# Gated attention in a two-model block: decays computed a head ahead, the gate's Silu behind the turned keys, state products first, level products mixed with eight blocks

## The reference, cut to what matters

```python
def gla_mixer(h, w_in, w_gate, b_gate, g_out, w_out):
    ...
    q, k, v, r, glr = jnp.split(proj, ...)
    log_a = jax.nn.log_sigmoid((glr @ w_gate + b_gate)) / GLA_TAU      # GLA_TAU = 16
    o = gla_chunked(q, k, v, log_a.reshape(B, S, H, DK))
    o = rmsnorm(o, g_out) * jax.nn.silu(r)
    return o.reshape(B, S, H * DV) @ w_out

def step(state, inp):                    # one chunk of gla_chunked
    qi, ki, vi, gi = inp
    b = jnp.cumsum(gi, axis=-2)
    o_inter = einsum(qi * exp(b), state)
    attn = einsum('bhik,bhjk,bhijk->bhij', qi, ki, exp(b_i - b_j, causal))
    o_intra = attn @ vi
    b_last = b[:, :, -1:, :]
    new_state = state * exp(b_last) + einsum(ki * exp(b_last - b), vi)
    return new_state, o_inter + o_intra
```

## Time and profile before

| | us |
|---|---|
| runs | 1488.01, 1482.47, 1490.82; median 1488.01 |
| profiled execution | 1484.64 |
| its span | 1482.9 |
| TensorE busy | 1389.9 (94%) |
| VectorE busy | 863.8 (58%) |
| ScalarE busy | 643.4 (43%) |
| TensorE's mean granted clock | 0.967 of full |

### The profile page before, as it was taken

How to read it: one execution, slowest core, us unless ns; L and a number is a source line. 1 busy time by engine, 2 the same in 40 slices (tenths; PEclk the granted TensorE clock), 3 DMA queues, 4 the chain that set the end, 5 groups by cost and what they waited for, 6 DMA issues and landing times.

```text
span 1482.9 us, 26632 instructions
## 1 busy us (share of the span) xinstructions
PE 1389.9 (94%) x9993; PEld 1267.9 (86%) x9993; DVE 863.8 (58%) x1635; ACT 643.4 (43%) x1171; POOL 14.9 (1%) x81
## 2 busy tenths in 40 slices
PE   5999999999999899999799987999999999899997
PEld 2988889888888799999677776999997778899996
DVE  0576667666533377777555544777775432775553
ACT  3455545455322255444554422545532332545542
POOL 4000000000000000000000000000000000000000
PEclk9899999999999999999999999899999999899998
DMA  8655446454491178879676822688797264476562
GB/s 303 187 154 159 131 125 185 143 156 144 126 304 53 42 216 261 265 218 296 180 225 201 250 63 65 183 262 271 226 281 264 91 166 121 133 224 182 155 185 86
DMA packets 400019, 270.00 MB, mean 182 GB/s; under 512 B 9914, under 2 KB 357424, under 8 KB 399936
## 3 DMA queue, kind: packets, MB, share of 16 engines
q1 hardware_dynamic: 399936, 268.83, 61.1%
HBM read 267.75 MB, written 1.05 MB: 181 GB/s over the span
## 4 chain that ended last, share of the span: by engine, by line
PE 84%; DVE 8%; ACT 4%; issue 2%; DMA 2%; SPq 1%; DVEq 0%; ACTq 0%
PE bank L738 18%; PE bank L739 18%; PE bank L740 17%; PE bank L724 6%; PE bank L792 4%; PE bank L695 2%; PE bank L1117 1%; DMA big<-in_w_ada 1%; PE bank L710 1%; PE bank L917 1%; PE bank L918 1%; PE bank L910 1%; PE bank L689 1%; DVE w_low L1789 1%; DVE h_parts L1805 1%
## 5 line engine op out<-in xcount | busy, mean ns | idle before, releaser
L738 PE MATMUL bank<-h_parts,w_high 128*128 128x256 f32 x1824 | 552.3, 303 | 17.1 <-DVE h_parts L1805 15.2
L739 PE MATMUL bank<-h_parts,w_high 128*128 128x256 f32 x1824 | 525.0, 288 | 0.0
L740 PE MATMUL bank<-h_parts,w_low 128*128 128x256 f32 x1824 | 524.4, 287 | 0.0
L1789 DVE TENSOR_TENSOR w_low<-w_raw,w_high 128x1024 fp32r<-128x1024 f32 (+2 forms) x324 | 362.0, 1124 | 108.6 <-ACT w_high L1310 96.9
L738 PEld LDWEIGHTS bank<-h_parts,w_high 128*128 128x128 f32 x1824 | 358.0, 196 | 35.3 <-issue 25.2
L739 PEld LDWEIGHTS bank<-h_parts,w_high 128*128 128x128 f32 x1824 | 359.6, 197 | 3.8 <-issue 3.5
L740 PEld LDWEIGHTS bank<-h_parts,w_low 128*128 128x128 f32 x1824 | 358.7, 197 | 0.0
L1310 ACT ACTIVATE w_high<-w_raw 128x1024 fp32r<-128x1024 f32 (+2 forms) x324 | 312.9, 973 | 63.4 <-PE bank L740 18.0
L738 PE MATMUL bank<-act_parts,w_high 128*128 128x256 f32 x528 | 150.1, 284 | 0.0
L1302 ACT ACTIVATE evac<-bank 128x256 f32<-128x256 f32 x140 | 53.9, 385 | 219.9 <-PE bank L740 195.9
L740 PE MATMUL bank<-act_parts,w_low 128*128 128x256 f32 x528 | 148.6, 281 | 0.0
(11 more groups left out here) (345 smaller groups left out, 1577.8 us busy)
## 6 DMA issues: line engine op xcount, KB each, us to landing
ada_w<-in_ada_w SPq DMA_DIRECT2D x48, 1024.0 KB, 6.2
w_raw<-in_ffn_w_in SPq DMA_DIRECT2D x88, 512.0 KB, 3.9
w_raw<-in_w_in SPq DMA_DIRECT2D x72, 512.0 KB, 3.9
w_raw<-in_w_ffn_in SPq DMA_DIRECT2D x44, 512.0 KB, 4.0
ada_w<-in_w_ada SPq DMA_DIRECT2D x16, 1024.0 KB, 7.1
w_raw<-in_gla_w_in SPq DMA_DIRECT2D x24, 512.0 KB, 6.4
w_raw<-in_ffn_w_out SPq DMA_DIRECT2D x32, 384.0 KB, 4.1
w_raw<-in_ffn_w_out SPq DMA_DIRECT2D x32, 320.0 KB, 3.6
```

Of the source, the lines that this page charges most:

```text
L738: pe.matmul(acc[:, 0:T], hi[:, n, :], x_parts[:, k, 0, :], start=k == 0, stop=False)
L739: pe.matmul(acc[:, 0:T], hi[:, n, :], x_parts[:, k, 1, :], start=False, stop=False)
L740: mm = pe.matmul(acc[:, 0:T], lo[:, n, :], x_parts[:, k, 0, :], start=False, stop=k == kb - 1)
L1789: dve.tensor_tensor(w_low[:, s, 0:m], w_raw[:, s, 0:m], w_high[:, s, 0:m].bitcast(F32), ALU.subtract)\
```

## The change

- VectorE's copy and subtractions become `decays(n)`. It is called once before the first head, and for head n + 1 in head n, behind the second state update (with a wait for it) and the low parts, before the wait for the norm. ScalarE's Exp becomes `decays(n)` too, called before the first head and then between the copy of block 5 and the Ln.
- VectorE computes `kd` before `qk2`.
- ScalarE's Silu and the two table loads move behind the copy of the turned keys.
- On TensorE the two state products (L1068) come before the level products. Block 3, eight k-steps, no longer follows them: one k-step is issued behind each of eight of the first eleven level products. `att_done` is signalled behind all of them.

```diff
                 products(G2)
                 rows2(1)
-                pe.wait_ge(S("scaled2"), 15 * (n - 1) + 2)
+                pe.wait_ge(S("scaled2"), 15 * (n - 1) + 1)
 ...
                 mm.then_inc(S("kd_turned"), 1)
                 products(G2)
                 rows2(2)
 
-                pe.wait_ge(S("scaled2"), 15 * n)
                 pe.wait_ge(S("tok2"), 2 * n)
-                for t in range(NT):
-                    for l in range(LEVELS):
-                        pe.matmul(bank[3 + t][:, l * CHUNK:(l + 1) * CHUNK], kt[:, l, tok[t]], qt[:, l, t, :], start=True, stop=True)
-                    mm = pe.matmul(bank[3 + t][:, 2 * T - 1:2 * T], qk2[:, tok[t]], ones[:, 0:1], start=True, stop=True)
-                mm.then_inc(S("att_done"), 1)
-
                 for c in range(2):
                     r = slice(c * CHUNK, (c + 1) * CHUNK)
                     if c == 1:
                         pe.wait_ge(S("kv_done"), 3 * (n - 1) + 1)
                     pe.matmul(bank[6][:, c * T:(c + 1) * T], kd_tok[r, 0, :], v_tok[r, 0, :], start=True, stop=True).then_inc(S("kv_done"), 1)
-                products(G2)
+                pe.wait_ge(S("scaled2"), 15 * n)
+                for t in range(NT):
+                    for l in range(LEVELS):
+                        pe.matmul(bank[3 + t][:, l * CHUNK:(l + 1) * CHUNK], kt[:, l, tok[t]], qt[:, l, t, :], start=True, stop=True)
+                        if t * LEVELS + l < NT * LEVELS - 1:
+                            products(1 if (t * LEVELS + l) % 3 < 2 else 0)
+                    mm = pe.matmul(bank[3 + t][:, 2 * T - 1:2 * T], qk2[:, tok[t]], ones[:, 0:1], start=True, stop=True)
+                mm.then_inc(S("att_done"), 1)
                 rows2(3)
 ...
@@ ScalarE
+            def decays(n):
+
+                act.wait_ge(S("expo"), 14 * n)
+                act.activation(expo, expo, ACT.Exp, scale=1.0 / TAU).then_inc(S("expo_done"), 1)
 ...
-                r = big[:, bass.ds(2 * i - 2, 2), :] if not isinstance(i, int) else big[:, 2 * i - 2:2 * i, :]
-                act.wait_ge(S("evacuated"), st_h2.done(i - 1, 1) + 3)
-                act.activation(r, r, ACT.Silu).then_inc(S("expo_done"), 1)
-                act.preload_act_table_set(LOG_EXP)
-                act.wait_ge(S("expo"), 14 * n)
-                act.activation(expo, expo, ACT.Exp, scale=1.0 / TAU).then_inc(S("expo_done"), 1)
 ...
                 act.activation(kd_tok.rearrange("p t d -> p (t d)"), bank[4][:, 0:NT * P], ACT.Copy).then_inc(S("tok2"), 1)
+                r = big[:, bass.ds(2 * i - 2, 2), :] if not isinstance(i, int) else big[:, 2 * i - 2:2 * i, :]
+                act.wait_ge(S("evacuated"), st_h2.done(i - 1, 1) + 3)
+                act.activation(r, r, ACT.Silu).then_inc(S("expo_done"), 1)
+                act.preload_act_table_set(LOG_EXP)
                 copies(5)
 ...
                 copies(6)
+                if gemm:
+                    decays(n + 1)
                 act.wait_ge(S("o2_sum"), n)
 ...
@@ VectorE
-                dve.tensor_tensor(qk2, q, k, ALU.mult).then_inc(S("scaled2"), 1)
-                dve.wait_ge(S("expo_done"), 2 * n)
+                dve.wait_ge(S("expo_done"), 2 * n - 1)
                 dve.tensor_tensor(kd, k, expo[:, 6 * T:7 * T], ALU.mult).then_inc(S("scaled2"), 1)
+                dve.tensor_tensor(qk2, q, k, ALU.mult).then_inc(S("scaled2"), 1)
 ...
                 if gemm and not last:
                     low(st_h2, i + 1, 0, IN_PARTS)
                     low(st_h2, i + 1, 1, IN_PARTS)
+                if gemm:
+                    dve.wait_ge(S("state2"), 3 * n)
+                    decays(i + 1)
                 dve.wait_ge(S("o2_rn"), 2 * n)
```

More of the change, by code:

```diff
@@ L1629, in _ @@
             head2(0, True, False)
+            decays(1)
             with act.Fori(1, H2 - 1) as i:
@@ L2190, in _, with decays @@
                 low(st_h2, 1, j, IN_PARTS)
-            def head2(i, gemm=True, last=False):
-                n, c = i, i - 1
-                cum = expo[:, 7 * T:8 * T]
+            cum = expo[:, 7 * T:8 * T]
+            def decays(n):
+                c = n - 1
                 dve.tensor_copy(cum, part(gb, c)).then_inc(S("expo"), 1)
@@ L2208, in head2 @@
                                   ALU.subtract).then_inc(S("expo"), 1)
+            def head2(i, gemm=True, last=False):
+                n, c = i, i - 1
                 dve.wait_ge(S("evacuated"), st_h2.done(c, 5) + 3)
                 q, k = qkv2[:, 0, :], qkv2[:, 1, :]
+                dve.wait_ge(S("expo_done"), 2 * n - 1)
+                dve.tensor_tensor(kd, k, expo[:, 6 * T:7 * T], ALU.mult).then_inc(S("scaled2"), 1)
                 dve.tensor_tensor(qk2, q, k, ALU.mult).then_inc(S("scaled2"), 1)
-                dve.wait_ge(S("expo_done"), 2 * n)
-                dve.tensor_tensor(kd, k, expo[:, 6 * T:7 * T], ALU.mult).then_inc(S("scaled2"), 1)
                 for l in range(LEVELS):
```

## The result

The changed kernel took 1500.76 us in the median of 4 runs (1499.91 to 1502.1), the kernel before 1485.45 us (1482.47 to 1490.82, 4 runs). The ratio is 1.0105 with a 95% interval of 1.0083 to 1.0127: slower by 15.6 us by the ratio, 15.3 between the medians. The forecast was 1500.7 us, +12.7, in a range of 1491 to 1507. One of the ten executions of `decays_ahead_only` further down (1494.86 us, at a mean granted clock of 0.915) fell into a slower state of the chip, and its ratio leaves it out. The profiled execution took 1502.1 us with a span of 1500.4, against 1484.64 and 1482.9.

A forecast was written before the change was run, and what follows sets the result against it. TensorE, on 84% of the chain that ended last, was taken to bound the kernel. Terms -6.5 -3.0 -2.9 +16.2 +4.8 +2.1 +1.45 +0.5 gave +12.7 us on 1488.0: 1500.7 us, range 1491 to 1507.

The forecast's parts named there:

- The new stalls: TensorE's waits for the state update before the third state product (L1074), four heads: 16.2 us of new idle.
- The third rival: State update not held behind the attention chain, so L1074 waits for nothing: -8.3 us, 1479.7 us; chance 0.10.
- the second: Rival: the stalls before L1074 come but the clock stays up: +7.4 us, 1495.4 us; chance 0.14.
- `kd`: Scaled keys in time in heads 2 and 3, 0.7 us to spare: -6.5 us idle, -3.0 us slow stretches.
- The fifth rival: kd still late behind gate product and weight split: +22 us if as late as before, else +13 to +15; chance 0.08.
- such loads: ScalarE's waits for next-head DMA loads: costed at nothing, at worst twice the 0.8 us waited before.
- The Exp before the norm: Exp ahead of the Ln delays head 4's start (L792): +1.45 us, plus 0.5 us for a possible slow stretch.
- The later Silu: ScalarE's Silu and table loads, 3.2 us, behind the turned keys: absorbed by ScalarE's waits, costed at nothing.
- The clock: Low clock behind the four stalls before L1074: 1.2 us each, +4.8 us in all, bounds 0 and 6.0.
- The joints: Extra late starts where block products follow level products, 21 joints at 0.1 us: +2.1 us, bounds 0 to 4.0.
- Mixing and the clock: Dense block products among the level products should end the slow stretches there in heads 2 and 4: -2.9 us.
- The fourth rival: Level products bring the low clock however mixed, 2.9 us not regained: +15.6 us, 1503.6 us; chance 0.10.

The follow-up runs named there:

- decays_ahead_only: The changed kernel with TensorE's old order (level products, att_done, two state products, block 3): 1477.24 us, ratio 0.9942 to the kernel before.
- update_ahead: The changed kernel with VectorE's state copy and first state update moved ahead of its wait for att_done: 1476.52 us, ratio 0.9928; run again, 1477.52 us.
- changed_unmixed: The changed kernel with block 3 put back in one piece behind the level products and att_done, state products still first: 1484.77 us, ratio 1.0003.
- tensor_order_only: The kernel before with only TensorE's new order (state products first, level products mixed with block 3): 1512.55 us, ratio 1.0164.
- ahead_unmixed: update_ahead with block 3 put back in one piece behind the level products and att_done: 1472.69 us, ratio 0.9892; run again, 1474.7 us.
- the pairs: Three mixed and unmixed comparisons on top of update_ahead; the unmixed kernel had the lower median by 2.8, 3.8 and 2.1 us.
- ahead_all: update_ahead with ScalarE's Exp behind the norm and the first head's decays ahead of that head's weight splits on VectorE: 1473.19 us, ratio 0.9888.

## Why the prediction was right, point by point

- **The new stalls** were forecast from the old chain at 4.69, 4.69, 5.72 and 3.8 us. They were 4.72, 4.72, 5.72 and 3.79. `update_ahead` and `changed_unmixed` show the cause from both sides: let the update out of the queue, or put the cover back, and they go. The third rival (the update is not held) is refuted, and so is the second (the clock stays up): 6.8 us of low clock go with each of the four.
- **`kd`** came in time in heads 2 and 3, as worked out. The fifth rival is refuted. Head 1's wait was not the 1.1 us left standing but 2.0. Its decays stand on VectorE behind a weight split, that split waits for ScalarE's rounding, and the rounding waits for a load; here before and after:

```profile
768.56 1.06 ACT L1310 ACTIVATE w_high<-w_raw 128x1024 fp32r<-128x1024 f32 x1 [0.17 <-DMA w_raw<-in_gla_w_in]
770.76 1.06 ACT L1310 ACTIVATE w_high<-w_raw 128x1024 fp32r<-128x1024 f32 x1 [1.81 <-DMA w_raw<-in_gla_w_in]
```

  Over the runs the wait for `kd` goes with this wait for the load, in `tensor_order_only` too, which has the old place of the decays: 0.17 us there and 1.09 for `kd` (before), 0.28 and 1.20 (`ahead_unmixed`), 0.64 and 1.56 (`changed_unmixed`), 1.56 and 2.06 (`tensor_order_only`), 1.81 and 1.98 (after). So the extra 0.9 us are not shown to come from the change; the prediction allowed 1.6 us in all for such loads. Why the load lands sooner or later is open.
- **The Exp before the norm** cost 1.26 us of wait at the start of head 4 (forecast 1.45), and a low clock behind it. The later Silu, costed at nothing, has no run of its own; no wait of TensorE for ScalarE appears in the changed kernel, and `decays_ahead_only`, which contains it, gains as expected.
- **The clock** is the term that was mis-sized. The step "I take all four new stalls as long enough, at 1.2 us each rather than 1.5" held as to whether and not as to how much. From the start of L1074 to the end of the block behind it, heads 1 to 4 took 3.70, 3.69, 3.61 and 4.18 us before and 6.03, 5.89, 6.13 and 6.56 after: +2.3, +2.2, +2.5 and +2.4, or 9.4 us in place of 4.8, since the low stretches were 6.8 us long and not 3.4. At L792 it was +1.6 in place of 0.5. Filling the stalls gave 8 us back. The bound of 1.5 us for a slow stretch, read from two stalls of 3.2 us, did not hold for stalls of 4 to 6.
- **The joints** were costed at +2.1 and came out at about -0.7 in all, if head 1's -0.22 is taken for three heads. Mixed, level products and block took 6.07 us in head 1 (784.24 to 790.31); apart they took 3.22 and 3.07. TensorE inside the mixed stretch of the changed kernel:

```profile
785.07 0.36 PE L738 MATMUL bank<-h_parts,w_high 128*128 128x256 f32 x1
785.27 0.28 PE L739 MATMUL bank<-h_parts,w_high 128*128 128x256 f32 x1
785.39 0.28 PE L740 MATMUL bank<-h_parts,w_low 128*128 128x256 f32 x1
785.51 0.55 PE L1065 MATMUL bank<-scratch 128*128 128x64 f32 x4
785.87 0.36 PE L738 MATMUL bank<-h_parts,w_high 128*128 128x256 f32 x1
```

  The 0.20 us from the first product to the second is there, as in the earlier trace rows. But the first product starts early, over the end of the small one: two level products take 0.36 us (785.51 to 785.87), where they take 0.46 in a run of their own.
- **Mixing and the clock.** "The mixing itself should end the slow stretches" came true in the changed kernel's profile, but it is no rule: the pairs gave no gain, and `ahead_all` shows the opposite case. The fourth rival, that the low clock comes however they are mixed, is no rule either (1 of 28 mixed heads). Whether mixing lowers the chance is open.
- **The sum.** Idle +12.0, clock +9.4 + 1.6 - 5.9, joints -0.7: +16.4, against 17.5 between the two spans, of which 1.3 us arose before the first head's first block was done, 0.7 of them in the wait for a load at L695. The forecast of +12.7 had the joints too high by 2.8, the clock too low by 5.7 and the idle time by 0.8; these errors partly cancel. That the absolute figure, 1500.7, met the measured 1500.76 is luck: the median of three runs that it started from, 1488.0, was 2.6 us above that of the four runs beside the changed kernel, and the +12.7 was as much too small (the medians are 15.3 apart).

Left open: why `update_ahead` and `changed_unmixed` came out some 4 to 5 us above the sums of their mechanisms. Part of it is scatter from outside the edited code: in the profiled executions the first head's values are turned (L1044) anywhere between 767.77 us and 776.12, before any of TensorE's edits. From there to the last L792 the heads take 139.2 us before, 155.3 changed, 131.5 in `decays_ahead_only`, 165.8 in `tensor_order_only`, 131.0 in `update_ahead` and 136.8 in `changed_unmixed`; each of these is one execution, with its own low clocks. `decays_ahead_only` alone ranged from 1470.72 to 1488.71 us over nine executions. And whether mixing helps or hurts by a microsecond or two, which 7 and 12 runs don't resolve.

## What to carry to other kernels

Moving a producer's work earlier helps only if its consumer is not queued behind something that you made later: follow the consumer's engine in program order up to the wait that you touch. Ahead of a signal, count what lies between it and the next wait of the same engine; that cover is what a long round trip through another engine lives on, and a block moved across the signal takes it away in full. And the clock has a price of its own: here stalls of 18.9 us in all, 3.8 to 5.7 each, cost another 9.4 us of slow products, about half as much again.

## What the runs showed of the hardware

- The low clock behind an idle stretch is not of one length. With 3.2 us of idle it lasted 3.4 us in the kernel before and 6.8 in `tensor_order_only`, at the same place of the program; with 3.8 to 5.7 us of idle before L1074 it was 6.8 us each time in the changed kernel, and part of it can pass while TensorE still idles (1.5 us of it in head 1).
- The same idle of 2.65 us had a low clock behind it at the start of head 4 in `tensor_order_only` and `ahead_all`, and none in the kernel before. Idle of 2.0 us had it in `update_ahead` (2.06) and not in the changed kernel (1.98), nor in `tensor_order_only` (2.06). So the length of the idle alone does not decide it.
- The clock can fall with TensorE nearly always busy: before 821.5 in the kernel before it was busy 3.44 of 3.50 us, with 64-column and half-height products. And it can stay low with no gap at all: 10.2 us in `ahead_all`, where the fall came behind a wait of 0.7 us.
- A 64-column level product in front of a 256-column one costs about 0.1 us less than in a run of its own (0.14 against 0.23 between starts), and the 256-column one behind it 0.08 us more (0.20 against 0.12).
